# Differential-attention heads: the context tiles first in every head, and the last row tile turned one head later

## The reference, cut to what matters

```python
q, k = apply_rope(q, cos, sin), apply_rope(k, cos, sin)      # image tokens only
k_all = concatenate([k, kc]); v_all = concatenate([v, vc])   # 768 keys for image queries
o1 = softmax(q[..., 0, :] @ k_all[..., 0, :].T * scale) @ v_all
o2 = softmax(q[..., 1, :] @ k_all[..., 1, :].T * scale) @ v_all
o = rms_norm(o1 - lam * o2, subln_g) * (1 - lam_init)
y = (o * silu(z)) @ w_out
# the same for the context: queries qc, keys kc and values vc alone (256 keys)
```

## Time and profile before

| | us |
|---|---|
| median of three runs | 1743.99 (1741.44 to 1747.99) |
| the profiled execution | 1752.03 |
| its span | 1750.7 |
| TensorE busy | 1597.8 (91%) |
| VectorE busy | 1104.7 (63%) |
| ScalarE busy | 623.1 (36%) |
| GpSimd busy | 627.8 (36%) |

### The profile page before, as it was taken

How to read it: one execution, slowest core, us unless ns; L and a number is a source line. 1 busy time by engine, 2 the same in 40 slices (tenths; PEclk the granted TensorE clock), 3 DMA queues, 4 the chain that set the end, 5 groups by cost and what they waited for, 6 DMA issues and landing times.

```text
span 1750.7 us, 21618 instructions
## 1 busy us (share of the span) xinstructions
PE 1597.8 (91%) x7933; PEld 1321.9 (76%) x7933; DVE 1104.7 (63%) x2135; ACT 623.1 (36%) x1505; POOL 627.8 (36%) x346
## 2 busy tenths in 40 slices
PE   5898899989998999989979999999997988899997
PEld 4786444787786788767778988888896766888886
DVE  6846665547776768897555555555555457665644
ACT  3213566231211120113433444443444346344431
POOL 6735000345654548464323033203324113332330
PEclk9998999999998999999999999999998999999999
DMA  5622000324433336563211011101102231111221
GB/s 176 190 63 94 1 1 1 133 92 127 135 108 112 117 98 231 167 206 91 92 49 37 13 49 49 30 19 49 49 24 73 100 105 49 49 49 31 67 85 48
DMA packets 115881, 142.55 MB, mean 81 GB/s; under 512 B 11048, under 2 KB 75200, under 8 KB 115776
## 3 DMA queue, kind: packets, MB, share of 16 engines
q1 hardware_dynamic: 89968, 91.77, 17.3%
q10 hardware_dynamic: 25808, 49.40, 8.5%
HBM read 132.74 MB, written 8.40 MB: 81 GB/s over the span
## 4 chain that ended last, share of the span: by engine, by line
PE 36%; DVE 8%; ACT 4%; issue 2%; ACTq 0%; DVEq 0%
PE ps L478 7%; PE ps L480 7%; PE ps L479 7%; PE ps L1156 3%; PE ps L1186 3%; PE ps L1377 2%; PE ps L1354 2%; PE ps L1172 1%; PE ps L1101 1%; PE ps L1366 1%; ACT tmp L1475 1%; DVE st L2772 1%; ACT p L2006 1%; DVE k_lo L2741 1%; DVE q L2740 1%
## 5 line engine op out<-in xcount | busy, mean ns | idle before, releaser
L466 POOL TENSOR_SCALAR w_hi<-w_raw 128x1024 fp32r<-128x1024 f32 x158 | 187.2, 1185 | 851.9 <-PE ps L480 651.2
L468 POOL TENSOR_TENSOR w_lo<-w_raw,w_hi 128x1024 fp32r<-128x1024 f32 x158 | 400.4, 2534 | 13.2
L478 PE MATMUL ps<-w_hi,h_hi 128*128 128x384 f32 (+2 forms) x768 | 284.8, 371 | 4.3 <-issue 2.6
L479 PE MATMUL ps<-w_lo,h_hi 128*128 128x384 f32 (+2 forms) x768 | 270.4, 352 | 0.0
L480 PE MATMUL ps<-w_hi,h_lo 128*128 128x384 f32 (+2 forms) x768 | 270.3, 352 | 0.0
L478 PE MATMUL ps<-h_hi,w_hi 128*128 128x512 f32 (+1 forms) x616 | 250.8, 407 | 10.3 <-POOL w_lo L468 6.3
L479 PE MATMUL ps<-h_lo,w_hi 128*128 128x512 f32 (+1 forms) x616 | 243.5, 395 | 0.0
L480 PE MATMUL ps<-h_hi,w_lo 128*128 128x512 f32 (+1 forms) x616 | 243.1, 395 | 0.0
L2501 DVE SCALAR_TENSOR_TENSOR mod_acc<-mod_piece,csil,mod_acc 128x512 f32<-128x512 f32 x140 | 201.1, 1476 | 23.4 <-DMA mod_piece<-in_ada_w 18.7
L478 PEld LDWEIGHTS ps<-w_hi,h_hi 128*128 128x128 f32 x768 | 149.6, 195 | 16.5 <-issue 3.5
L479 PEld LDWEIGHTS ps<-w_lo,h_hi 128*128 128x128 f32 x768 | 149.5, 195 | 9.5 <-issue 0.2
(11 more groups left out here) (320 smaller groups left out, 2826.1 us busy)
## 6 DMA issues: line engine op xcount, KB each, us to landing
mod_piece<-in_ada_w ACTq DMA_DIRECT2D x96, 256.0 KB, 3.1
w_raw<-in_w_gate_up SPq DMA_DIRECT2D x88, 256.0 KB, 3.2
w_raw<-in_a_w_in SPq DMA_DIRECT2D x128, 128.0 KB, 2.3
w_raw<-in_w_down SPq DMA_DIRECT2D x22, 512.0 KB, 4.0
w_raw<-in_b_w_in SPq DMA_DIRECT2D x20, 512.0 KB, 3.7
w_raw<-in_w_out SPq DMA_DIRECT2D x16, 512.0 KB, 3.8
w_raw<-in_w_in SPq DMA_DIRECT2D x8, 512.0 KB, 3.7
w_raw<-in_w_o SPq DMA_DIRECT2D x8, 512.0 KB, 3.8
```

Source lines behind the costliest of these rows:

```text
L466: pool.tensor_scalar(hi, raw, 1.0, 0.0, ALU.mult, ALU.add).then_inc(*s["pool_step"].up())
L468: pool.tensor_tensor(lo, raw, hi, ALU.subtract).then_inc(*s["w_split"].up(pair))
L478: pe.matmul(out, a[0], b[0], start=start, stop=False)
L479: pe.matmul(out, a[0], b[1], start=False, stop=False)
```

## The change

- One order, HEAD_TILES = 4, 5, 0, 1, 2, 3, serves attention and projection in every head; the projection runs 4, 5, 0, 1, z, z, 2, 3. FIRST_ORDER and `last_tile` go.
- A head's last tile, 3, is no longer turned at the end of the head before, but beside chunk 6 of the next head's first product (tile 4 of the head after), in n = 2 of its own attention. The scores wait for it at n = 4, where the first image tile begins; scores 0 wait for tile 5 alone. The other turns are one product behind their own, as before, except that none stands beside tile 2 (tile 1 is turned beside the first z).
- HEAD_FILL gives 3, 3, 4, 4 chunks beside the short units, which are now the first four, and 6 beside each long one.
- The tables of head 7 follow the new order, with as many chunks in all.
- The values of pair 0 are now the context's (four matmuls) and those of pair 1 image tiles' (twelve); their PSUM places are swapped accordingly. In `act_head_rows` the wait for the values of two heads back stands at the first tile of the order.

```diff
-LAST_GATE = {0: (4,), 1: (2, 2), 2: (4,), 3: (2, 2)}
-LAST_AHEAD = {5: (1, 1), 6: (2,), 7: (2,), 8: (3,), 9: (3,), 10: (3,), 11: (2, 1)}
+LAST_GATE = {0: (4,), 1: (2, 2), 2: (4,), 3: (4,)}
+LAST_AHEAD = {5: (2,), 6: (2,), 7: (1, 1), 8: (3,), 9: (2, 1), 10: (3,), 11: (2, 1)}
-HEAD_TILES = (0, 1, TX, TX + 1, 2, 3)
-HEAD_FILL = (4, (2, 1), 6, (3, 2), 6, (3, 2), 6, (5,), 6, (5,), 6, (3, 2))
+HEAD_TILES = (TX, TX + 1, 0, 1, 2, 3)
+HEAD_FILL = (3, (2, 1), 4, (4,), 6, (6,), 6, (3, 3), 6, (3, 3), 6, (3, 3))
+def turned_beside(unit, c):
+    kind, hd, t = unit
+    if c != TURN_AT:
+        return None
+    i = HEAD_TILES.index(t) if kind == "row" else None
+    if kind == "row":
+        return (hd - 1, HEAD_TILES[-1]) if i == 0 else (hd, HEAD_TILES[i - 1]) if i != TX else None
+    if t == 0:
+        return (hd, HEAD_TILES[-1]) if hd == 7 else (hd + 1, HEAD_TILES[TX - 1])
+    return None
 def beside_units(hd):
-    rows = [("row", hd + 1, t) for t in range(TA)] if hd < 7 else []
+    rows = [("row", hd + 1, t) for t in HEAD_TILES] if hd < 7 else []
     return rows[0:TX] + [("z", hd, j) for j in range(2)] + rows[TX:]
 def tile_before(hd, t):
+    i = HEAD_TILES.index(t)
+    return (hd, HEAD_TILES[i - 1]) if i > 0 else (hd - 1, HEAD_TILES[-1]) if hd > 0 else None
 def pe_heads_first(k, pe):
-    for t in FIRST_ORDER[4:]:
-        pe_head_turn(k, pe, 0, t)
+    pe_head_turn(k, pe, 0, HEAD_TILES[-2])
 def pe_beside(k, pe, hd):
-            if c == TURN_AT and kind == "row" and 0 < t != TX:
-                pe_head_turn(k, pe, h, t - 1)
-            if c == TURN_AT and kind == "z" and t == 0 and h < 7:
-                pe_head_turn(k, pe, h + 1, TX - 1)
+            if turned_beside(unit, c) is not None:
+                pe_head_turn(k, pe, *turned_beside(unit, c))
             yield
-    if hd < 7:
-        pe_head_turn(k, pe, hd + 1, TA - 1)
 def pe_head_values(k, pe, hd, pair):
-    out = (k.ps[:, 2, 0:256], k.ps[:, 3, 0:256], k.ps[:, 2, 256:512])[pair]
-    chunks = range(TX, TA) if pair == 1 else range(TA)
+    out = (k.ps[:, 3, 0:256], k.ps[:, 2, 0:256], k.ps[:, 2, 256:512])[pair]
+    chunks = range(TX, TA) if pair == 0 else range(TA)
 def pe_heads(k, pe):
-        pe.wait_ge(*s["head_ready"].at((hd, last_tile(hd))))
+        pe.wait_ge(*s["head_ready"].at((hd, TX + 1)))
         for n in range(12):
+            if n == 2 * TC:
+                pe.wait_ge(*s["head_ready"].at((hd, HEAD_TILES[-1])))
             pe_head_scores(k, pe, hd, n)
```

More of the change, by code:

```diff
@@ L589, in beside_units @@
 def beside_units(hd):
-    rows = [("row", hd + 1, t) for t in range(TA)] if hd < 7 else []
+    rows = [("row", hd + 1, t) for t in HEAD_TILES] if hd < 7 else []
     return rows[0:TX] + [("z", hd, j) for j in range(2)] + rows[TX:]
 def bank_order():
-    units = [("row", 0, 3)]
+    units = [("row", 0, HEAD_TILES[-1])]
     for hd in range(8):
@@ L1048 @@
 EARLY = {TX: 0, TX + 1: 2, 0: 1, 1: 3, 2: 4}
-FIRST_ORDER = (TX, TX + 1, 0, 1, 2, 3)
 def tile_before(hd, t):
[L1054 to L1061, removed]
+    i = HEAD_TILES.index(t)
+    return (hd, HEAD_TILES[i - 1]) if i > 0 else (hd - 1, HEAD_TILES[-1]) if hd > 0 else None
 def pe_heads_first(k, pe):
@@ L1085, in pe_heads_first @@
     pe.wait_ge(*s["turn_tmp"].at(("h6", TX + 1, 1)))
-    for i, t in enumerate(FIRST_ORDER[2:]):
-        pe_head_turn(k, pe, 0, FIRST_ORDER[i])
+    for i, t in enumerate(HEAD_TILES[2:]):
+        pe_head_turn(k, pe, 0, HEAD_TILES[i])
         row(t)
-    for t in FIRST_ORDER[4:]:
-        pe_head_turn(k, pe, 0, t)
+    pe_head_turn(k, pe, 0, HEAD_TILES[-2])
 def pe_head_turn(k, pe, hd, t):
@@ L1252, in pe_out0_chunk @@
         elif (t, nh) == (0, 1):
-            pe.wait_ge(*s["head_ready"].at((7, TA - 1)))
+            pe.wait_ge(*s["head_ready"].at((7, HEAD_TILES[-1])))
         elif (t, nh) in ((1, 1), (2, 0)):
@@ L1937, in act_head_rows @@
         act.copy(k.rot[:, :, :, :], x.to_broadcast([P, 4, 2, HD])).then_inc(*s["head_plain"].up((hd, t)))
-    if hd >= 2 and t == 0:
+    if hd >= 2 and t == HEAD_TILES[0]:
         act.wait_ge(*s["head_valued"].at((hd - 2, 2)))
@@ L1956, in act_beside @@
         for c in range(KD):
[L1957 to L1960, removed]
+            if turned_beside(unit, c) is not None:
+                act_head_turned(k, act, *turned_beside(unit, c))
             if c < KD - 1:
@@ L1971, in act_beside @@
         yield
-    if hd < 7:
-        act_head_turned(k, act, hd + 1, TA - 1)
 def act_head_rstd(k, act, hd):
@@ L2022, in act_heads @@
     s = k.sig
-    act_head_rows(k, act, 0, FIRST_ORDER[0])
+    act_head_rows(k, act, 0, HEAD_TILES[0])
     act_gate_turn_out(k, act, TX - 2)
     act_gate_turn_out(k, act, TX - 1)
-    for i, t in enumerate(FIRST_ORDER):
+    for i, t in enumerate(HEAD_TILES):
         if i > 0:
             act_head_rows(k, act, 0, t)
-            act_head_turned(k, act, 0, FIRST_ORDER[i - 1])
-    act_head_turned(k, act, 0, FIRST_ORDER[-1])
+            act_head_turned(k, act, 0, HEAD_TILES[i - 1])
     act.wait_ge(*s["gate_out"].at(2))
@@ L2749, in dve_beside @@
         for c in range(KD):
[L2750 to L2753, removed]
+            if turned_beside(unit, c) is not None:
+                dve_head_turned(k, dve, *turned_beside(unit, c))
             if c < KD - 1:
@@ L2762, in dve_beside @@
         yield
-    if hd < 7:
-        dve_head_turned(k, dve, hd + 1, TA - 1)
 def dve_head_least(k, dve, hd, n):
@@ L2807, in dve_heads @@
     dve_gate_turn_out(k, dve, TX - 1)
-    for i, t in enumerate(FIRST_ORDER):
+    for i, t in enumerate(HEAD_TILES):
         dve_head_rows(k, dve, 0, t)
         if i > 0:
-            dve_head_turned(k, dve, 0, FIRST_ORDER[i - 1])
-    dve_head_turned(k, dve, 0, FIRST_ORDER[-1])
+            dve_head_turned(k, dve, 0, HEAD_TILES[i - 1])
     dve.wait_ge(*s["x_out"].at(("4", TX - 1)))
```

## The result

| | before | after |
|---|---|---|
| median of 20 runs each, us | 1745.25 (1739.28 to 1755.22) | 1751.56 (1742.90 to 1758.89) |
| ratio to before, 95% interval | | 1.0039 (1.0024 to 1.0054) |
| profiled execution, its span, us | 1752.03, 1750.7 | 1748.66, 1747.3 |
| heads 1 to 6, us | 355.0 | 371.5 |

The change costs 6.3 us by the medians and 4 to 9 us by the interval: real, and under the 0.5% that was set as the bound, so it counts as no change. The profiled execution of after is 3.4 us shorter than that of before all the same. It reached the first scores at 890.77 instead of 906.30; 5.4 us of that is the change's, the other 10.1 lie in the stages ahead, whose instructions the change doesn't touch (between 400 and 600 us the mean granted clock was 0.91 in the profiled execution of before and 0.97 in that of after). From here on I therefore compare head with head.

What follows compares the result with a forecast made beforehand. TensorE, busy 91%, bounds the kernel. Head 0 −10.2, heads 1 to 6 +2.0, head 7 +1.1, clock +9.8 sum to +2.7 on 1743.99: 1747 us; own range 1739 to 1753, full range 1727 to 1760.

Steps and rivals of the forecast that it cites:

- the term for the clock: TensorE's granted clock: half of 14 new stall places fall to the lower level, 1.4 us each, +9.8 us.
- the waits for k_lo go: TensorE's turns and scores: waits for the keys' low half, 11.2 and 11.9 us, go; work untouched.
- The floor of 53.2 us a head: TensorE's work in one head without any wait, worked out from head 3: about 53.2 us.
- Opening: At n = 0, 1: tile 3's rope delays scores(1), the mix delays transposes; losses 2.0 and 0.8 us.
- Mid-head: At n = 5 to 7: 1/rms block on ScalarE delays tile 0's rope and turn; 3.4 us together.
- the walk: One head of 1 to 6 followed through its queues, full clock: 59.5 us each, 357.0 together, +2.0.
- the signs: Expected in the trace after, among others: a 2.4 us wait at L1101, about 5 us behind scores(5).
- Head 0: First scores 5.4 us earlier, no previous head's work: 50.9 us long, −10.2 us.
- Head 7: Gains up to n = 4, draws to n = 6, then loses: +1.1 us.
- The two rules weighed: In the 1/rms block: one shared table load would give 1739; 1.38 us drain per load, 1764.
- The case for another block length: Rival, 1/rms block on ScalarE: one load less gives 1739, 2.8 us longer gives 1764; chance 0.01.
- the clock falls at nearly every stall: Rival at the two new stalls a head: about 12 falls of 14, +12 us, 1756; chance 0.25.

Runs made afterwards that it cites:

- experiment 8: After with 1/rms block behind filler's reads, last tile's rope behind first mix, HEAD_FILL starting 5, (1, 1), 3: 1703.54 us, ratio 0.9774 to before.
- Experiment 2: After with rope of a head's last tile behind the next head's first reduce and mix on VectorE: 1735.66 us, ratio 0.9952 to before.
- experiment 3: After with HEAD_FILL starting 5, (1, 1), 3, (4,), more chunks beside the first unit: 1746.05 us, ratio 1.0013 to before.
- Experiment 1: After with the previous head's 1/rms block behind the filler's reads at n = 5 on ScalarE: 1730.82 us, ratio 0.9916 to before.
- experiment 5: After with 1/rms block behind filler's reads and last tile's rope behind first reduce and mix: 1710.97 us, ratio 0.9820 to before.
- Experiment 4: After with HEAD_FILL's old numbers of chunks, the new order of tiles kept: 1731.32 us, ratio 0.9934 to before.
- move 1: The edit to after that puts the 1/rms block behind the filler's reads at n = 5 on ScalarE; alone 1730.82 us, ratio 0.9916 to before.
- experiment 7: After with 1/rms block behind filler's reads, last tile's rope behind first mix, HEAD_FILL starting 4, (2, 1), 3: 1707.89 us, ratio 0.9795 to before.

## Why the prediction was right, point by point

The forecast was 1747 us, +2.7 on 1743.99, with its own range 1739 to 1753; 1751.56, +6.3, was measured, near the upper end of that range. Both stalls came where and as long as foreseen; the term for the clock was too small. By its steps:

- **Nothing of the work changes, the waits for k_lo go**: so they did, 23.1 us of them. The floor of 53.2 us a head is a little low: experiment 8 took 54.3, of which TensorE was busy 53.8.
- **Opening**: scores(1) were to come 3.85 us behind scores(0), with 1.9 idle, and the transposes to wait 0.65. They came at 3.83, 1.86 and 0.74. Experiment 2 ties the first to the rope on VectorE, experiment 3 to the length of the cover.
- **Mid-head**: the turn of tile 0 was to wait 2.4, and did, 2.44 (six times, 14.7 us in all). From scores(5) to scores(8) 18.45 us were foreseen; 18.71 were taken. Experiment 1 ties it to the block's place. TensorE began to wait 8.2 us behind scores(5) (1220.66 in head 5), as the walk has it (7.96), and not the "about 5" that the signs name.
- **Head 0**: −10.2 foreseen (50.9 long), −10.1 measured (51.01), all of it from a last turn that nobody waits for.
- **Head 7**: +1.1 foreseen, +1.5 measured. Scores(4) come 15.11 us behind scores(0) (15.1 foreseen), scores(7) 19.78 behind those (19.2), scores(11) 18.62 further on (18.8). With its share of the clock term, 1.4, the forecast for this head was 1.0 too high.
- **The two rules weighed**: the block runs 1215.62 to 1219.88, again 4.26 us with two loads, 1.28 each, and neither a load saved nor a drain. The case for another block length has nothing for it.
- **Head lengths** of 59 to 62 us: four of the six were; heads 1 and 2 took 63.31 and 62.12.

**What was mis-sized is the clock.** At full clock the sum gives 6 × 59.5 = 357.0 us for heads 1 to 6, with the clock term 365.4; they took 371.5. By the stretches of after and experiment 1 that stayed at the full clock, a head with both stalls takes 59.7, so 1.2 us are the walk's own error. One microsecond is something that I hadn't costed (below). The other 12.2 are clock. I let half the places fall at 1.4 each, 8.4 us for these six heads, because the new waits seemed a little lighter than the old; but all six openings fell, where four had in before, and three of the six mid-head places besides. The windows of after show it: the opening of head 5 from scores(1) on, 4.87 us where the one opening of experiment 1 that stayed at the full clock (head 2, with the same waits) took 3.54; head 4 from scores(6) to scores(7), 9.00 us at a mean clock of 0.81, against 7.83 for the same stretch of head 5 at the full clock. Between the levels, 0.50 and 1.00, the mean of a stretch tells how much of it lay at the lower one.

```profile
1194.27:1199.14 4.87, 4.12 (x17) 3.83 (x18) 1.49 (x3) 1.38 (x4) 0.00 (x0) 0.65 0.27 76
1155.46:1164.46 9.00, 6.56 (x31) 6.03 (x31) 5.47 (x12) 5.13 (x11) 0.00 (x0) 0.81 0.00 1
1217.17:1225.00 7.83, 5.39 (x32) 4.76 (x31) 4.30 (x11) 4.50 (x9) 0.00 (x0) 1.00 0.00 0
```

The six openings cost 9.7 us (2.7 for head 1, 1.0 to 1.6 each for the others), the three mid-head places 0.7 to 0.9 each by scores(9), since behind a slower stretch TensorE no longer waits for the exp at scores(8): 12.2 together. The term should have been 4 us larger, and the result stands between my forecast and the rival "the clock falls at nearly every stall". That rival was right on the openings and wrong on mid-head. The Trainium skill's account of a clock that swings where TensorE idles briefly but often (TensorE: Matmul & The Clock Gate, "A second HAM failure mode: psum-queue depth-cycling") gave the direction: this trace agrees in that three waits a head brought nine falls in heads 1 to 6 where two waits a head brought four there in before, and in that with the rope's and the turn's wait taken away (experiment 5) none fell in these heads. Less idle time didn't always mean fewer falls, however (experiment 3).

**What the prediction didn't say** is that the two halves of the change have opposite signs. I walked the new numbers of chunks through the queues and found the mid-head wait, but put it down to the order: a long exp ahead of the block where a context tile's had been. Experiment 4 shows that with the old numbers the same order has no such wait. A walk of each half alone could have shown it.

Where the time of after lies, then, by the ratios on 1745 us: the order of tiles with the old numbers −11.5 (head 0's start, and some 6 us in heads 1 to 6, 348.9 against 355.0), the numbers of chunks +18. The mid-head wait with its clock falls accounts for that within the intervals: move 1, which removes it and keeps the numbers, brings back 21.5.

Left open: which waits make the clock fall. The idle time of a place doesn't tell it, as the last section shows, and no run here changes a wait without changing what lies around it.

## What to carry to other kernels

When work is dealt out between the steps of another engine's loop, the number of pieces in each step decides behind which instruction of the other engines' queues each hand-over lands: count, for every hand-over, what stands ahead of it in each queue, and put long blocks that nobody waits for (here 4.3 us of 1/rms) behind the reads that free or feed TensorE. Change the order and the counts one at a time, because a gain of one can hide in the other's loss. Price the slower clock behind a stall as well as the stall: here, over six heads, it cost 12 us beside 32 us of idle time (371.48 − 339.50).

## What the runs showed of the hardware

**The granted clock doesn't follow the idle time of one place.** Idle time of head 5 by the timeline, and how often the mean clock of the stretch behind it was under 1.00, heads 1 to 6 of one trace each:

| kernel | opening idle, us | openings fallen | mid-head idle, us | mid-heads fallen |
|---|---|---|---|---|
| after | 1.86 + 0.74 | 6 | 2.44 | 3 |
| experiment 1 | 1.94 + 0.74 | 5 | none | 0 |
| experiment 2 | 0.23 + 1.08 | 0 | 2.44 | 3 |
| experiment 3 | 0.82 + 0.74 | 5 | 2.46 | 6 |
| experiment 4 | 0.21 + 1.63 + 0.74 | 3 | none | 0 |
| experiment 5 | 0.21 + 0.87 | 0 | none | 0 |

With less idle time in the opening, experiment 3 had more falls in all than after, 11 against 9; the same 2.4 to 2.5 us in mid-head fell in three, three and six heads of six. In head 6 the wait for the mix was 2.66 us in experiment 2, 2.08 in experiment 5 and 2.15 in experiment 7: only the last fell (0.75 from scores(1) to scores(2)). Before shows it most plainly: with the same waits, 1.2 and 1.7 us, ahead of each of its openings 1 to 6, these took 5.28, 4.45, 3.06, 5.28, 4.45 and 3.06 us, at mean clocks of 0.50, 0.62, 1.00, 0.50, 0.62 and 1.00. Why equal waits end so differently is not shown. A fall cost from 0.7 us (mid-head, net) to 2.7. The mean clock of all executions of a kernel goes the same way as the falls of its one trace: 0.956 for after and experiment 3, 0.958 for experiment 1, 0.962 and 0.963 for 2 and 4, 0.964 to 0.965 for 5 to 8.

**VectorE operations were held up by GpSimd.** In the opening of head 6 of after the rope's L2721 took 1.44 us, where it takes 0.42 to 0.50 in the openings of the other heads, while GpSimd, 1.18 us late for a DMA, was still in the last of its splits. VectorE's timeline, then GpSimd's:

```profile
1253.46 1.44 DVE L2721 TENSOR_TENSOR rot<-rot,rot6b 128x256 f32<-128x256 f32 x1
```

```profile
1251.11 1.05 POOL L466 TENSOR_SCALAR w_hi<-w_raw 128x1024 fp32r<-128x1024 f32 x1 [1.18 <-DMA w_raw<-in_a_w_in]
1252.24 2.37 POOL L468 TENSOR_TENSOR w_lo<-w_raw,w_hi 128x1024 fp32r<-128x1024 f32 x1
```

The operation ended at 1254.90, 0.29 us behind GpSimd's 1254.61. As the first exp, and with it scores(1), stands behind the rope, this is the 1.0 us of head 6 that the sum lacked.

The same happens in every head at a place where nobody waits for it. The new order puts the rope of tile 2 beside the splits, some 7 us before the head's end. There its last two operations (L2721, L2723) took 1.75 and 1.15 us instead of 0.42 and 0.43 (1.75 and 1.28 in head 0). VectorE and GpSimd at the end of head 4:

```profile
1183.69 1.75 DVE L2721 TENSOR_TENSOR rot<-rot,rot6b 128x256 f32<-128x256 f32 x1
```

```profile
1182.21 2.95 POOL L468 TENSOR_TENSOR w_lo<-w_raw,w_hi 128x1024 fp32r<-128x1024 f32 x1
```

That is 2.0 us of VectorE a head, most of the 14 that heads 1 to 6 have more of it than before (213.7 against 199.4, 396 instructions in both). Over the heads of all ten traces, each of these two operations that took over 0.8 us ended 0.26 to 0.30 us behind the GpSimd instruction that it ran beside. So each was held until that instruction was through, and the price depended on who waited: no wait of TensorE is listed for it at the end of a head, 1.0 us was lost in the opening of head 6. The operation of the earlier trace rows (L2782) has one wide operand and two columns of scalars, and not two wide ones as the prediction's "two SBUF operands" suggests; the same operation took 2.60 us instead of 0.68 in the opening of head 6 of experiment 2.
